# Moving a recurrent branch, page sums, a sample turn and closing norms within a hybrid decoder step

## The reference, cut to what matters

```python
def recurrent_branch(xr, xg, conv_prev, h0, ...):
    xc, conv_new = causal_dwconv(xr, conv_prev, w_conv, b_conv)
    r = sigmoid(xc @ w_r + b_r); i = sigmoid(xc @ w_i + b_i)     # block by block
    log_a = LRU_C * r * log_sigmoid(lam)
    a = exp(log_a);  u = sqrt(-expm1(2.0 * log_a)) * i * xc
    h[t] = a[t] * h[t-1] + u[t]
    return h * gelu(xg), h_last, conv_new

def decoder_layer(x, c, ...):
    sh1, sc1, g1, sh2, sc2, g2 = split(silu(c) @ w_ada + b_ada, 6)
    fq, fk, fv, fg, sq, sk, sv, xr, xg = split((x * (1 + sc1) + sh1) @ w_in)
    fox = fox_attention(fq, fk, fv, cumulative log forget gates)      # softmax
    sb = stick_breaking_attention(sq, sk, sv)
    lru = recurrent_branch(xr, xg, ...)
    x = layer_norm(ALPHA * x + g1 * (concat([fox, sb, lru]) @ w_out), ln1_g, ln1_b)
    ua, ub = split((x * (1 + sc2) + sh2) @ w_up)
    ffn = (gelu(causal_dwconv(ua)) * ub) @ w_down
    return layer_norm(ALPHA * x + g2 * ffn, ln2_g, ln2_b), new states
```

## Time and profile before

| | |
|---|---|
| Median of 3 runs | 1529.51 us (1529.25 to 1535.27) |
| Profiled execution: time, span | 1532.5 us, 1530.9 us |
| Granted TensorE clock over the span | 0.978 |
| PE busy | 1461.1 us (95%) |
| DVE busy | 841.4 us (55%) |
| ACT busy | 403.5 us (26%) |
| POOL busy | 79.4 us (5%) |
| Line with the largest share of the chain | PE L2214 (FFN up), 44% |

### The profile page before, as it was taken

How to read it: one execution, slowest core, us unless ns; L and a number is a source line. 1 busy time by engine, 2 the same in 40 slices (tenths; PEclk the granted TensorE clock), 3 DMA queues, 4 the chain that set the end, 5 groups by cost and what they waited for, 6 DMA issues and landing times.

```text
span 1530.9 us, 25633 instructions
## 1 busy us (share of the span) xinstructions
PE 1461.1 (95%) x9800; PEld 1309.1 (86%) x9800; DVE 841.4 (55%) x1321; ACT 403.5 (26%) x729; POOL 79.4 (5%) x111
## 2 busy tenths in 40 slices
PE   6999999899999999899899999999999999999996
PEld 3768887666556777699799999999999999999996
DVE  3406787995566665834654444444443545444566
ACT  2212434444454575613432100001000000010011
POOL 0233000000000000002300000000000000000013
PEclk8999999999999999999999999999999999999997
DMA  9765862765872112331111112111111111211122
GB/s 342 254 217 181 240 192 89 227 195 154 255 248 72 49 44 84 127 108 48 55 50 47 34 42 62 42 55 38 40 46 56 53 32 35 67 46 41 35 83 93
DMA packets 179295, 159.99 MB, mean 105 GB/s; under 512 B 12171, under 2 KB 158231, under 8 KB 179202
## 3 DMA queue, kind: packets, MB, share of 16 engines
q1 hardware_dynamic: 146596, 141.15, 29.3%
q10 hardware_dynamic: 30566, 17.50, 3.9%
q0 software_dynamic: 2048, 0.20, 0.2%
HBM read 142.25 MB, written 13.79 MB: 102 GB/s over the span
## 4 chain that ended last, share of the span: by engine, by line
PE 84%; DVE 8%; ACT 4%; issue 3%; DMA 1%; ACTq 1%; SPq 0%; POOL 0%; DVEq 0%
PE ps L2214 44%; PE ps L1960 15%; PE ps L2163 6%; PE ps L2021 3%; PE ps L2061 3%; PE ps L2329 2%; PE ps L2043 2%; PE ps L2075 1%; PE ps L1883 1%; PE ps L2263 1%; DVE k_page L873 1%; PE ps L1889 1%; PE ps L2222 1%; PE ps L2025 1%; DVE pr L942 1%
## 5 line engine op out<-in xcount | busy, mean ns | idle before, releaser
L2214 PE MATMUL ps<-acts_lo,w_hi 128*128 128x344 f32 x1008 | 213.9, 320 | 0.0
L2214 PE MATMUL ps<-acts_hi,w_hi 128*128 128x344 f32 x1008 | 213.8, 320 | 0.0
L2214 PE MATMUL ps<-acts_hi,w_lo 128*128 128x344 f32 x1008 | 212.8, 319 | 0.0
L1960 PE MATMUL ps<-acts_hi,w_hi 128*128 128x344 f32 (+1 forms) x552 | 184.1, 333 | 6.8 <-DVE scores L854 3.0
L1180 DVE CAST w_hi<-w_raw 128x1024 fp32r<-128x1024 f32 x72 | 50.6, 702 | 239.8 <-PE ps L2214 227.6
L1960 PE MATMUL ps<-acts_hi,w_lo 128*128 128x344 f32 (+1 forms) x552 | 177.5, 321 | 0.0
L1960 PE MATMUL ps<-acts_lo,w_hi 128*128 128x344 f32 (+1 forms) x552 | 177.4, 321 | 0.0
L2214 PEld LDWEIGHTS ps<-acts_lo,w_hi 128*128 128x128 f32 x1008 | 170.6, 189 | 0.0
L2214 PEld LDWEIGHTS ps<-acts_hi,w_hi 128*128 128x128 f32 x1008 | 169.7, 188 | 0.0
L2214 PEld LDWEIGHTS ps<-acts_hi,w_lo 128*128 128x128 f32 x1008 | 167.9, 188 | 0.0
L1850 ACT ACTIVATE ffn_cols<-ps 128x10 f32 x22 | 4.0, 180 | 447.4 <-PE ps L2214 447.3
(11 more groups left out here) (334 smaller groups left out, 2370.8 us busy)
## 6 DMA issues: line engine op xcount, KB each, us to landing
w_ada<-in_w_ada SPq DMA_DIRECT2D x12, 2048.0 KB, 8.9
w_raw<-in_w_up SPq DMA_DIRECT2D x44, 512.0 KB, 3.8
k_page<-in_cache_fox_k SPq DMA_DIRECT2D x64, 192.0 KB, 3.1
k_page<-in_cache_sb_k SPq DMA_DIRECT2D x64, 192.0 KB, 3.0
k_page<-in_cache_fox_v SPq DMA_DIRECT2D x64, 192.0 KB, 2.8
k_page<-in_cache_sb_v SPq DMA_DIRECT2D x64, 192.0 KB, 3.5
w_raw<-in_w_in ACTq DMA_DIRECT2D x15, 512.0 KB, 6.5
w_raw<-in_w_down SPq DMA_DIRECT2D x16, 384.0 KB, 3.3
```

The lines of the kernel that those rows point to most:

```text
L1960: last = nc.tensor.matmul(bank[0:cols, 0:CH], w[:, n % 2, k, 0:cols], a[:, k, c * CH:(c + 1) * CH], start=k == 0 and w is w_hi and a is ac ...
L2214: last = nc.tensor.matmul(proj_ps[half][:, c, 0:CH], w[:, half, k], a[:, k, c * CH:(c + 1) * CH], start=k == 0 and w is w_hi and a is hi, ...
```

## The change

- Page sums: reduction 9 of the second attention goes from slot 21 to 22.
- Recurrence: the second convolution input (x 2) is projected ahead of k 5 and v 5, G1 goes from 64 to 62, and tile 1's gate gets a row of its own in `lru`. Gelu goes to slot 68, its products to 69, the splits to 70 (tile 0) and 71 (tile 1). The row turns "ks" and "vs" go from 58 and 61 to 59 and 66. VectorE's weight splits and decode output go from 67 to 68. The early output projection also takes k = 6 and 7: (0, 1) with k 0 to 4 at 70, then at 72 its k 6, 7 and (0, 0), at 73 (1, 1), at 75 (1, 0), each without k = 5, which is done behind the loop.
- Sample rows: TensorE turns them behind m = 7 of pass 2 instead of 5, and VectorE takes two more casts first.
- Norm 2: in the last pass norms stand behind m = 0, 2, 4, each scale step one norm later than before, and the very last step runs in two halves of 512 columns with a store each.

```diff
@@ -116,7 +116,7 @@
         stM.close()
         mix_lo = sbA("mix_lo", [P, 512], F32R)
         stL = ExitStack()
-        lru = stL.enter_context(nc.sbuf_tensor("lru", [P, 5, TOK], F32))
+        lru = stL.enter_context(nc.sbuf_tensor("lru", [P, 6, TOK], F32))
         stL.close()
         scores = sbA("scores", [P, 2, NPG, NB, H])
         WA = W + 8
@@ -157,7 +157,7 @@
         lru_rows = smp_rows[0:RWS, 0:DL]
         XR_BUF = (lru[:, 0], lru[:, 4])
         XC_BUF = (lru[:, 1], lru[:, 0])
-        RG_BUF = (lru[:, 2], misc[:])
+        RG_BUF = (lru[:, 2], lru[:, 5])
         IG_BUF = (lru[:, 3], lru[:, 4])
         HS_BUF = RG_BUF
         XG_BUF = (lru[:, 1], lru[:, 3])
@@ -341,8 +341,8 @@
                     ("k", 2), ("v", 2),
                     ("k", 3), ("v", 3),
                     ("k", 4), ("v", 4),
-                    ("x", 0), ("k", 5), ("v", 5),
-                    ("x", 2), ("x", 1), ("x", 3)]
+                    ("x", 0), ("x", 2), ("k", 5), ("v", 5),
+                    ("x", 1), ("x", 3)]
         PHASES = [7, 4, 2, 2, 2, 3, 3]
         NIN = len(IN_TILES)
         assert sum(PHASES) == NIN and WT == 3 and TT == 8
@@ -438,12 +438,12 @@
         for r in range(4, 2 * NB):
             RED_AT.setdefault(r - 4, []).append(r)
         for r in range(2 * NB):
-            RED_AT.setdefault(SB_K + 7 * r // 8, []).append(2 * NB + r)
+            RED_AT.setdefault(SB_K + r - (r > 0) - (r > 9), []).append(2 * NB + r)
         SB_Z = SB_K + 14
         V_AT = SB_Z + 4
-        G0, G1 = LATE + 5, LATE + 14
+        G0, G1 = LATE + 5, LATE + 12
         AFTER = {16: "bias", 18: "kf", 19: "peak", 21: "level", 24: "own", 26: "vf", SB_Z + 2: "tail",
-                 LATE + 8: "ks", LATE + 11: "vs", X1_AT + 9: "lru"}
+                 LATE + 9: "ks", LATE + 16: "vs", X1_AT + 9: "lru"}
         BEFORE = {}
         NSET = 2 * NPG
         for n in range(NSET):
@@ -521,6 +521,9 @@
         DAT = {tt: n for n, tt in enumerate(DORDER)}
         ND, LAST_Y = len(DSPANS), len(DORDER) - 2
 
+        Y_AT = {1: (1, 3, 5, 7), 2: (0, 2, 4)}
+        Y_SCALE = {(1, 3): 0, (1, 5): 1, (1, 7): 2, (2, 0): 3, (2, 2): 4, (2, 4): 5, (2, 5): 6}
+
         def tok_cols(tt):
             return slice(tt * P, tt * P + P) if tt < TT else slice(SEQ, TOK)
 
@@ -531,8 +534,9 @@
             return (psA[:, 0], psB[:, 0], psT[:, 0], psT[:, 1])[n % 4] if n < KT else (psA[:, 0], psB[:, 0], psA[:, 1], psA[:, 2])[n % 4]
 
         EARLY = {(0, 1): psB[:, 2], (0, 0): psA[:, 0], (1, 1): psB[:, 0], (1, 0): psA[:, 2]}
-        EARLY_K = range(2 * WT - 1)
-        EARLY_AT = {NU - 2: [(0, 1)], NU: [(0, 0), (1, 1)], NU + V_LAG - 1: [(1, 0)]}
+        HEADS, GATED = (*range(2 * WT - 1),), (2 * WT, 2 * WT + 1)
+        EARLY_AT = {NU - 2: [(0, 1, HEADS)], NU: [(0, 1, GATED), (0, 0, HEADS + GATED)], NU + 1: [(1, 1, HEADS + GATED)],
+                    NU + V_LAG - 1: [(1, 0, HEADS + GATED)]}
 
         def out_bank(c, m):
             if (c, m) in EARLY:
@@ -728,15 +732,21 @@
             for n, tt in enumerate(DORDER):
                 if n < LAST_Y:
                     sp.wait_ge(y_o, n + 1)
+                elif n == LAST_Y:
+                    sp.wait_ge(y_z, 1)
                 else:
-                    sp.wait_ge(y_z, n - LAST_Y + 1)
+                    for half in range(2):
+                        cols = slice(D // 2 * half, D // 2 * half + D // 2)
+                        sp.wait_ge(y_z, 2 + half)
+                        sp.dma_start(y_rows_d[:, tt, cols], y_tile[n % 3][:, cols]).then_inc(y_s[n % 3], 16)
+                    continue
                 if tt < TT:
                     sp.dma_start(y_rows_d[:, tt], y_tile[n % 3]).then_inc(y_s[n % 3], 16)
                 else:
                     sp.dma_start(o["y_sample"][:, 0], y_tile[n % 3][0:NB]).then_inc(y_s[n % 3], 16)
 
             for n in range(3):
-                sp.wait_ge(y_s[n], 16 * 3)
+                sp.wait_ge(y_s[n], 16 * (3 + (n == (len(DORDER) - 1) % 3)))
             sp.wait_ge(y_fs, 96)
             sp.wait_ge(s_lr, 64)
             sp.wait_ge(s_cc, 32)
@@ -1158,12 +1168,13 @@
                         RV["scan", t] = rd
                 for t in range(LT):
                     x = HS_BUF[t]
-                    if g == NU + 1:
+                    if g == NU - 3:
                         dve.wait_ge(r_s, 11)
                         rstep(V.tensor_tensor(x, x, XG_BUF[t], ALU.mult))
-                    if g == NU + 2:
+                    if g == NU - 2 + t:
                         rstep(V.tensor_copy(acts_hi[:, 2 * WT + t], x))
                         rstep(V.tensor_tensor(acts_lo[:, 2 * WT + t], x, acts_hi[:, 2 * WT + t].bitcast(F32), ALU.subtract))
+                        RV["acts", t] = rd
 
             def mix_low(n):
 
@@ -1207,7 +1218,7 @@
                     reduce(r)
                 take_after(g)
                 lru_step(g)
-                if g == NU - 5:
+                if g == NU - 4:
                     dve.wait_ge(s_pm, DENSE_END)
                     for m in range(2):
                         g_split(m, m, 1)
@@ -1317,9 +1328,9 @@
             h2_hi(1, range(2))
             for j in range(2):
                 g_split(KT + j, j, KT // 2 + 1)
-            h2_hi(1, range(2, 4))
+            h2_hi(1, range(2, 6))
             sample_norm()
-            h2_hi(1, range(4, KT))
+            h2_hi(1, range(6, KT))
             for tt in TILES[2]:
                 norm_tile(AT[tt], tt)
             h2_hi(2)
@@ -1461,19 +1472,18 @@
                 V.reciprocal(st[:, 15:16], st[:, 14:15]).then_inc(y_d, 1)
                 dve.wait_ge(y_d, at + 4)
                 dve.wait_ge(y_g, n + 1)
-                V.scalar_tensor_tensor(out=y, in0=y, scalar=st[:, 15:16], in1=ln2b, op0=ALU.mult, op1=ALU.add).then_inc(y_z, 1)
+                for cols in ((slice(0, D),) if n == LAST_Y else (slice(0, D // 2), slice(D // 2, D))):
+                    V.scalar_tensor_tensor(out=y[:, cols], in0=y[:, cols], scalar=st[:, 15:16], in1=ln2b[:, cols],
+                                           op0=ALU.mult, op1=ALU.add).then_inc(y_z, 1)
 
             for c in range(1, ND):
                 at = [DAT[tt] for tt in DTILES[c - 1]]
                 for m in range(KT):
                     down_add(c, m)
-                    if m == 0 and c == 2:
-                        scale2(DAT[DTILES[0][3]])
-                    n = (m - 1) // 2
-                    if m % 2 == 1 and n < len(at):
-                        norm2(at[n])
-                    elif m % 2 == 0 and m and n < len(at):
-                        scale2(at[n])
+                    if m in Y_AT[c]:
+                        norm2(at[Y_AT[c].index(m)])
+                    if (c, m) in Y_SCALE:
+                        scale2(Y_SCALE[c, m])
             for n in range(LAST_Y, len(DORDER)):
                 norm_last(n)
 
@@ -1602,8 +1612,6 @@
 
                 g, t, c = "ri".index(name[0]), int(name[1]), int(name[2])
                 act.wait_ge(s_pm, JOB[name] + 1)
-                if (g, t, c) == (0, 1, 0):
-                    act.wait_ge(t_m, 2 * TURN["v", NP2 - 1] + 2)
                 at = (A_BR, A_BI)[g] + t
                 A.activation((RG_BUF, IG_BUF)[g][t][:, c * CH:c * CH + CH], ps_dense[:, 0:CH], ACT.Sigmoid,
                              bias=vecT[:, at:at + 1]).then_inc(s_pe, 1)
@@ -1655,7 +1663,7 @@
                         act.wait_ge(r_s, 4 * t + 4)
                         A.activation(RG_BUF[t], RG_BUF[t], ACT.Sqrt, scale=-1.0).then_inc(r_s, 1)
                         A.activation(XC_BUF[t], XC_BUF[t], ACT.Sqrt).then_inc(r_s, 1)
-                if g == NU:
+                if g == NU - 4:
                     act.wait_ge(s_pe, DENSE_END)
                     A.activation(lru[:, 1:4:2], lru[:, 1:4:2], ACT.Gelu_apprx_tanh).then_inc(r_s, 1)
 
@@ -2157,11 +2165,12 @@
             def out_mms(c, m, ks):
 
                 a, b = SPANS[c]
+                end = 2 * WT - 1 if (c, m) in EARLY else KT - 1
                 for k in ks:
                     hi, lo = (w_hi[:, m, k], w_lo[:, m, k]) if m < 2 else (wo_hi[:, m - 2, k], wo_lo[:, m - 2, k])
                     for w, act in ((hi, acts_hi), (hi, acts_lo), (lo, acts_hi)):
                         last = nc.tensor.matmul(out_bank(c, m)[:, 0:b - a], w, act[:, k, a:b],
-                                                start=k == 0 and w is hi and act is acts_hi, stop=k == KT - 1 and w is lo)
+                                                start=k == 0 and w is hi and act is acts_hi, stop=k == end and w is lo)
                 return last
 
             def out_early(g):
@@ -2171,12 +2180,14 @@
                     pe.wait_ge(s_mx, 32)
                     pe.wait_ge(o_l, 2)
                 elif g == NU:
+                    pe.wait_ge(b_z, NU - 1 - HALF_U)
+                    pe.wait_ge(r_d, RV["acts", 1])
+                elif g == NU + 1:
                     pe.wait_ge(b_z, NU - HALF_U)
-                for c, m in EARLY_AT[g]:
```

(17 more changed lines are left out.)

## The result

The changed kernel takes **1536.43 us**, median of 8 runs (1533.91 to 1540.22), beside 1530.1 (1526.8 to 1535.27) for the kernel before on the same chip: ratio **1.0039**, 95% interval 1.002 to 1.0058, some 6 us slower. The profiled execution took 1536.45, 1.55 more than its span of 1534.9.

The account below looks back on a forecast made before the run. TensorE bounds the kernel (84% of the last-ending chain); only its idle or slow-clock time can be gained. Page sums -0.3, recurrence +7.1, sample rows -3.2, end -3.4 sum to +0.2: 1529.7 us beside the median, range 1516 to 1538.

Parts of the forecast that it names:

- Recurrence: Gates, scan and early output projection: +7.1 us, from +5.9 delay at slot 72 and +1.2 of half clock.
- The half clock: Behind the new wait at slot 72: 2.45 us lost to half clock instead of 1.3, so +1.2.
- The two moved row turns … cost nothing: Turns "ks" and "vs" in their new slots: no cost, dense multiplications there cover ScalarE; without cover, about 1.02 us each.
- The lower bound of +4.7: Recurrence: +4.7 us if tile 1's split came at the same time but TensorE's clock held.
- The upper bound of +10: Recurrence: +10 us if the roots end 2 to 3 us later, evictions standing behind new table loads.
- First rival: Wait at slot 72 hidden, VectorE's chain about 5 us sooner or TensorE later: total -10 to -16 us, chance 0.24.
- Second rival: Recurrence's roots slip by a slot, moving VectorE's chain about 8.9 us: total +9, 1538.6 us, chance 0.10.
- Table switches: ScalarE in the recurrence: six table loads instead of five, 1.28 us each, without the skill's 1.38 us drain.
- Sample rows: Turn two output tiles later: 3.24 us stall goes, last norms bind next; -3.2 us, between -2.0 and -3.7.
- End: Closing norms and stores: shorter scale-step waits, TensorE stall and last store; -3.4 us, between -1.7 and -4.3.
- shrinks to about 2: End: TensorE's stall of 4.08 us at 1517.23, ahead of its last turns, falls to about 2.
- Page sums: Reduction 9 one slot later: 3.60 us stall ends, new 3.5 us stall follows; -0.3 us, between -2.2 and +0.5.

Follow-up runs that it names:

- e4: Whole change, with only the early projection's ungated k 0 to 4 in slot 72 and its gated products in slot 74; ratio 0.9987 to the kernel before.
- e1: Kernel before with the recurrence part of the change alone; ratio 1.0066 to the kernel before.
- e7: Whole change, with tile 1's scan behind unit 67's weights, Gelu from slot 68 to 69, mix_low behind the scan; ratio 1.0012 to the kernel before.
- e8: Whole change without its page sums part, with the edits of e3, e4 and e7; 1522.79 us, ratio 0.9934 to the kernel before.
- e5: Kernel before with the page sums part alone (reduction 9 one slot later); ratio 0.9992 to the kernel before.
- e2: Kernel before with page sums, sample rows and end parts, without the recurrence part; ratio 0.9984 to the kernel before.
- e3: Whole change, with the last scale step on VectorE behind m = 7 of the last pass instead of m = 5; ratio 1.0014 to the kernel before.

## Why the prediction was right, and where it was wrong

By the medians the number was off by 6 us. In the four stretches, which leave out the page sums, the forecast adds up to +0.5 and the profile to +4.9. Two terms make the difference: the recurrence is 2.8 worse than forecast and the end 2.0; the sample rows give back 0.4. That the result lies in the range is owed to its width more than to the sum.

**Recurrence: mechanism right, term mis-sized, +7.1 against about +10.** The chain on VectorE was worked out as 28.5 and took 28.36 (610.65 to 639.01). TensorE's delay at slot 72, counted from the last dense product, was worked out as +5.9 and is +6.0 (639.11 - 607.92, against 632.15 - 606.96). The half clock was taken as +1.2 and is about +1.0: the block there is 27 multiplications and not 30 as I wrote (fifteen heads and twelve gated), 7.15 us, where fifteen and twelve at the full clock take 5.06 in e4 (from 641.80 and 648.62); that is 2.1 lost, and 1.1 was lost before (30 in 6.69, against 5.6 at that rate). That this size came out is luck in part. The 4.9 us were counted from the end of the 3.07 stall to 634.77, but the clock there was 1.00 until 631.0 and 0.50 only from 631.3 to 634.5; and in the whole change the lower level began inside the wait, 1.9 us ahead of the first multiplication. What I missed is the rest:

- *"The two moved row turns … cost nothing"*, because *"the slots they go to are full of dense multiplications that cover ScalarE"*, is the step that failed. It also let the sum begin at slot 72, as if nothing ahead of it moved. In stretch a TensorE's busy time grows by 0.42 and its idle time by 1.45 (90.61 - 88.15 to 92.48 - 88.57). Of that 1.27 is in waits for ScalarE, which add up to 2.44 before and 3.71 after. The two moved turns and two of the gate products stand open, as TensorE's timeline of the whole change shows, with the turn of slot 58 in the kernel before ahead of it:

```profile
542.21 0.49 PE L1980 MATMUL ps<-ident,smpT 128*8 128x128 f32 x3
```

```profile
546.20 1.09 PE L2069 MATMUL ps<-w_raw,tok 128*64 128x128 f32 x16
548.39 0.49 PE L1988 MATMUL ps<-ident,smpT 128*8 128x128 f32 x3 [1.10 <-ACT misc L1576]
...
571.96 0.85 PE L2130 MATMUL ps<-lru,gate_w 128*128 128x344 f32 x2 [0.42 <-ACT lru L1616]
581.38 0.84 PE L2130 MATMUL ps<-lru,gate_w 128*128 128x344 f32 x2 [0.41 <-ACT lru L1616]
...
602.18 0.49 PE L1988 MATMUL ps<-ident,smpT 128*8 128x128 f32 x3 [0.22 <-ACT lru L1569]
```

  ScalarE's timeline of the whole change in slot 59:

```profile
546.95 1.04 ACT L1660 ACTIVATE lru<-lru 128x1032 f32<-128x1032 f32 x1
547.90 0.44 ACT L1576 ACTIVATE misc<-ps 128x344 f32<-128x344 f32 x1
```

  Row turns, gate products and dense pieces share one bank, and each waits until the product before it was evicted (`aux`, `pe.wait_ge(s_pe, JOB[name])`). In slots 59 and 66 ScalarE's exponential and tanh of a tile (L1659, L1660; slot G + 4) stand ahead of that eviction, and behind the dense piece only the values are left to cover it (1.09 at 546.20). So the turns' waits, 1.10 and 0.22, come with the slots that they were moved to; tile 0's exponential in slot 59 was not moved at all. Two gate products of tile 1 have a turn of two and of four blocks between them, which is too short to cover the sigmoid (0.42 and 0.41; with six blocks at 588.20 there is no wait); before there was one such (0.42 at 601.10). A wait of 0.46 at 551.53 went. That is the 1.27: 1.10 + 0.22 + 0.42 + 0.41 - 0.42 - 0.46. The price without cover, one pass of ScalarE (1.02), was near for the first turn; the error was to take the cover for given. That a comes with the recurrence part is shown by e1, e4, e7 and e8 (92.49 to 92.51 in each, 90.61 to 90.65 without); the row turns were not tried without the gates' move. The sentence that ScalarE *"has its sigmoids and its Gelu done ahead of it"* held for VectorE's chain, which waited for nothing.
- Behind the early projection b grows by another 1.0: TensorE has waits of 0.3 and 0.15 for ScalarE at a bank used again, the rest is in the multiplications.

The lower bound of +4.7 rested on a clock that holds; it did not. The upper bound of +10 was reached, by other work than the one it was set for.

**First rival.** It needed VectorE's chain about 5 us sooner. The order of the program kept it from that, as the text against it said. e7 shows that the reorder alone gives 3.3; e4 shows that the wait goes more cheaply on TensorE's side, which the prediction did not see as a way. **Second rival:** the roots did not slip: 610.65, as forecast (609.6) but for the last dense product, which ended 0.96 later. **Table switches:** 1.28 each with the next activation 0.01 behind; the drain that the Trainium skill ("ScalarE: Activation LUTs", section "What ACT_TABLE_LOAD costs") gives is not in these rows either, so keeping the row's price was right.

**Sample rows: -3.2 forecast, -3.63 in c**, inside the bounds. The wait of 3.24 went, and the last norms start 3.63 earlier, counted from the start of the pass. Against e1 and e5, which have the code of before there, the gain is 3.8 and 2.6, so the sum is borne out and its last half us is not decided.

**End: -3.4 forecast, -1.38 in the profile** and -2.27 and -2.33 in e2 and e4, the same code. The failed step is *"shrinks to about 2"* with *"the first eight of the sixteen transposes take about 1.0"*: I added one scale step at its 1.23, and did not look at what GpSimd would be doing beside it. It took 3.21 and the wait was 3.11. The second half of the step had a wrong ground: that no shorter wait was followed by half clock was read from the eight transposes right behind one, and the clock falls later than that (see the last section; a wait of 2.05 in the trace of before was followed by it). Behind the same wait of 3.11 the sixteen turns took four different times, TensorE's timelines of the whole change, e7, e4 and e2 show (the first stands above, 3.37):

```profile
1514.28 3.67 PE L2234 MATMUL ps<-ident,resT 128*128 128x128 f32 x16 [3.11 <-DVE resT L1424]
```

```profile
1519.78 2.40 PE L2232 MATMUL ps<-ident,resT 128*128 128x128 f32 x16 [3.11 <-DVE resT L1423]
```

```profile
1515.42 1.97 PE L2230 MATMUL ps<-ident,resT 128*128 128x128 f32 x16 [3.11 <-DVE resT L1421]
```

In e4 and e2 the first eight, for which VectorE waits, run at the full clock, in the other two at half; d falls into the same two pairs (32.54 and 32.60, 33.49 and 33.44). With the scale step moved, d gains 4.39, which the bound of -4.3 nearly held. The halves of the last store are as forecast: 512 KB land in 2.6, 256 KB in 2.0, and from the last step's start to the end of the span there are 4.0 us instead of 4.4 (-0.4 against -0.3).

**Page sums: -0.3 forecast, not told apart from 0** (e5), and the stalls changed places as worked out, 2.73 + 1.25 for the 3.5 named. What the clock costs there differs more from profile to profile than the forecast term (0.78 to 0.91 over that stretch). The 2.3 us of half-clock time that it took behind the old stall are too few even for the trace of before: the clock is 0.50 from 310.5 to 317.0, with TensorE busy throughout, which loses some 3.3.

## What to carry to other kernels

When work is made earlier, ask first what the consumer's program waits for at that place: a wait ahead of work that does not need it costs all of itself, and putting the independent multiplications first (e4, 5.8 us of b) gave more than speeding up the producer (e7, 3.7). A cover is read instruction by instruction at the slot that something moves to: what stands between it and the product before it, and what the evicting engine does there. And before a VectorE step is moved, look at what GpSimd runs beside its new place: 1.22 us can become 3.21.

## What the runs showed of the hardware that was not expected

A VectorE addition of two SBUF operands ended 1.08 us after the end of the GpSimd addition beside it, in the whole change, e3, e4, e7 and e8 alike, while VectorE steps that read PSUM kept their length. And the granted clock: how long TensorE waited does not alone decide which level follows. Waits of 1.88 (e4) and 2.28 (e8) were followed by the lower of its two levels for 3.4 us, a wait of 2.25 in the kernel before (615.36) by the full clock to the next wait; behind the same 3.11 at the end the clock was 0.50 in e7, 0.79 in e4 and 1.00 in e2 over the sixteen turns. Nor does the fall come at the wait: behind a wait of 2.05 in the kernel before, eight transposes still ran at the full clock, as the busy time of the stretch behind it shows:

```profile
281.87:282.90 1.03, 1.03 (x10) 0.86 (x10) 1.03 (x1) 0.28 (x1) 0.00 (x0) 1.00 1.17 360
283.10:286.00 2.90, 2.90 (x20) 1.83 (x20) 2.80 (x7) 0.61 (x2) 0.00 (x0) 0.50 1.01 297
```

So whether a wait cost clock is read from the granted clock of the stretch behind it, and not from the first instructions. What decides the level is not shown by these runs.
